# Query low parts in 128-row columns, and linear-attention outputs by pairs of chunks

## The reference, cut to what matters

```python
scores = jnp.einsum('bhtk,bhsk->bhts', q_rel, k_rel)
scores = jnp.where(causal, scores, 0.0)
o = (jnp.einsum('bhts,bhsv->bhtv', scores, vi)
     + jnp.einsum('bhtk,bhkv->bhtv', qi * jnp.exp(b), state))
new_state = (jnp.exp(b_end[..., 0, :])[..., None] * state
             + jnp.einsum('bhsk,bhsv->bhkv', k_end, vi))
```

```python
s = jnp.einsum('bqhd,bshd->bhqs', qb, kk).astype(jnp.float32) * scale
...
a = probs(qb1, k1) - lam * probs(qb2, k2)
return jnp.einsum('bhqs,bshv->bqhv', a.astype(v.dtype), v)
```

## Time and profile before

| | us |
|---|---|
| median of 3 runs | 3016.75 |
| lowest, highest | 3014.66, 3020.86 |
| the profiled execution | 3015.33 |
| its span, first to last instruction | 3013.4 |
| TensorE busy | 2768.4 (92%) |
| VectorE busy | 1497.1 (50%) |
| ScalarE busy | 1224.0 (41%) |
| GpSimd busy | 580.2 (19%) |

### The profile page before, as it was taken

The page is one execution under the profiler, slowest core; times in us unless marked ns, Lnnn a source line. Parts: engine busy times, 40 slices in busy tenths (PEclk is TensorE's granted clock), DMA queues, the critical chain, the costliest instruction groups (busy, mean ns, idle before and its releaser), DMA issues. The chain is left out here.

```text
span 3013.4 us, 36775 instructions
## 1 busy us (share of the span) xinstructions
PE 2768.4 (92%) x13602; PEld 2274.7 (75%) x13602; DVE 1497.1 (50%) x2280; ACT 1224.0 (41%) x1954; POOL 580.2 (19%) x479
## 2 busy tenths in 40 slices
PE   7999999988988599999996699689998999999999
PEld 6887766766767588888885688578876888888887
DVE  4670363456422588888885768456624211221121
ACT  4111243555522278777774411466523312222130
POOL 3222111100221012222221322000022322222221
PEclk9999999999999599999998899799999999999999
DMA  4133124210532299999995511000031211111112
GB/s 149 49 99 114 46 69 130 85 32 24 160 121 97 110 359 376 392 380 372 375 367 207 176 50 32 15 1 1 1 112 56 61 52 49 49 42 56 49 49 77
DMA packets 139399, 380.18 MB, mean 126 GB/s; under 512 B 25984, under 2 KB 49280, under 8 KB 114688
## 3 DMA queue, kind: packets, MB, share of 16 engines
q1 hardware_dynamic: 122032, 344.76, 32.8%
q0 software_dynamic: 10656, 20.99, 2.0%
q10 hardware_dynamic: 6576, 12.58, 1.2%
HBM read 346.81 MB, written 49.28 MB: 131 GB/s over the span
## 5 line engine op out<-in xcount | busy, mean ns | idle before, releaser
L412 POOL TENSOR_TENSOR w_lo<-w_raw,w_hi 128x512 fp32r<-128x512 f32 (+2 forms) x312 | 390.1, 1255 | 1576.4 <-ACT w_hi L387 1575.5
L387 ACT ACTIVATE w_hi<-w_raw 128x512 fp32r<-128x512 f32 (+2 forms) x312 | 184.3, 601 | 975.0 <-PE banks L461 947.4
L2142 DVE TENSOR_TENSOR w_lo<-w_raw,w_hi 128x2048 fp32r<-128x2048 f32 x192 | 436.5, 2290 | 65.8 <-ACT w_hi L2078 60.4
L2078 ACT ACTIVATE w_hi<-w_raw 128x2048 fp32r<-128x2048 f32 x187 | 355.9, 1926 | 39.3 <-PE banks L2199 39.3
L461 PE MATMUL banks<-w_hi,act_hi 128*128 128x512 f32 (+1 forms) x768 | 295.6, 385 | 22.9 <-POOL w_lo L412 10.6
L461 PE MATMUL banks<-act_hi,w_hi 128*128 128x512 f32 x768 | 300.8, 392 | 8.6 <-DVE act_lo L266 3.7
L461 PE MATMUL banks<-act_lo,w_hi 128*128 128x512 f32 x768 | 299.6, 390 | 0.0
L461 PE MATMUL banks<-act_hi,w_lo 128*128 128x512 f32 x768 | 299.5, 390 | 0.0
L461 PE MATMUL banks<-w_hi,act_lo 128*128 128x512 f32 (+1 forms) x768 | 294.4, 383 | 0.0
L461 PE MATMUL banks<-w_lo,act_hi 128*128 128x512 f32 (+1 forms) x768 | 294.4, 383 | 0.0
L2197 PE MATMUL banks<-w_hi,xT 128*128 128x512 f32 x512 | 205.9, 402 | 1.4 <-DVE xT L2147 1.4
(11 more groups left out here) (462 smaller groups left out, 5214.7 us busy)
## 6 DMA issues: line engine op xcount, KB each, us to landing
w_raw<-in_w SPq DMA_DIRECT2D x192, 1024.0 KB, 7.6
w_raw<-in_w_in SPq DMA_DIRECT2D x96, 256.0 KB, 2.7
w_raw<-in_w_up SPq DMA_DIRECT2D x72, 256.0 KB, 2.8
w_raw<-in_w_down SPq DMA_DIRECT2D x64, 256.0 KB, 2.8
scratch_gateT<-gate_staged SPq DMA_DIRECT2D x32, 256.0 KB, 2.2
gate<-scratch_gateT SPq DMA_DIRECT2D x32, 256.0 KB, 3.4
w_raw<-in_w_out SPq DMA_DIRECT2D x32, 256.0 KB, 3.3
y_rows<-scratch_y SPq DMA_DIRECT2D x8, 1024.0 KB, 8.9
```

The lines of the kernel that those rows point to most:

```text
L387: act.activation(v.w_hi[:, i % RING, :cols], v.w_raw[:, i % RING, :cols], ACT.Copy).then_inc(hi_done, 1)
L412: pool.tensor_tensor(v.w_lo[:, i % RING, :cols], v.w_raw[:, i % RING, :cols], v.w_hi[:, i % RING, :cols].bitcast(F32), ALU.subtract).then_ ...
L2078: act.activation(hi[c % SLOTS][:, :], raw[c % TILES][:, :], ACT.Copy).then_inc(hi_done, 1)
L2142: dve.tensor_tensor(lo[c % SLOTS][:, :], raw[c % TILES][:, :], hi[c % SLOTS][:, :].bitcast(F32), ALU.subtract).then_inc(lo_done, 1)
```

## The change

In the differential attention `q_lo` gets the layout of `q_dup`: for each side a full 128-row column in which the other side's 64 rows are zero. The second matmul of `split_scores` then takes 128 rows of `q_lo` and of `k_both`; the rows that would meet the keys' low part are multiplied by zero. POOL writes the zeros in four memsets (64 partitions x 512 elements each, one waiting for the other) at the start of the stage, before its gate subtractions, and the first scores of blocks 0 and 1 wait for them. The larger `q_lo` takes room from the row buffers: one slot instead of two, so only block 0's rows are loaded in the stage before, block 1's at the stage's start after block 0 is turned, and block i + 2's after block i + 1 is turned.

In the linear attention the outputs go by pairs of chunks: both score matmuls, then both state matmuls, where it was score, state, score, state.

```diff
-    v.dq_rows = at("dq_rows", FREE + 103, [P, 2, DA_W])
-    v.dk_rows = at("dk_rows", FREE + 107, [P, 2, DA_W])
+    v.dq_rows = at("dq_rows", FREE + 107, [P, DA_W])
+    v.dk_rows = at("dk_rows", FREE + 109, [P, DA_W])
...
-                    for c in range(8 * half, 8 * half + 8):
-                        r, tt = chunk_rows(c), c // 2
-                        out = v.bank[6 + half][r, (tt % 4) * P:(tt % 4 + 1) * P]
-                        mm = pe.matmul(out, scT[r, h % 2, tt, :], v.hv[r, tt, hc], start=True, stop=(c == 0))
-                        if c:
-                            pe.wait_ge(state_done, NCH * h + c)
-                            mm = pe.matmul(out, q_dec[h % 2][:, c * CHUNK:(c + 1) * CHUNK], st[:, c - 1, :], start=False, stop=True)
+                    mine = range(8 * half, 8 * half + 8)
+                    for tt in range(4 * half, 4 * half + 4):
+                        pair = (2 * tt, 2 * tt + 1)
+                        for c in pair:
+                            r = chunk_rows(c)
+                            pe.matmul(out_of(c), scT[r, h % 2, tt, :], v.hv[r, tt, hc], start=True, stop=(c == 0))
+                        for c in pair:
+                            if c:
+                                pe.wait_ge(state_done, NCH * h + c)
+                                mm = pe.matmul(out_of(c), q_dec[h % 2][:, c * CHUNK:(c + 1) * CHUNK], st[:, c - 1, :], start=False, stop=True)
...
-    q_lo = [at(f"q_lo{i}", q_at[i] + 4, [P, DA_H, P], F32R) for i in range(2)]
+    q_lo = [at(f"q_lo{i}", q_at[i] + 4, [P, 2, DA_H, P], F32R) for i in range(2)]
...
-                if h == 2 and i + 2 < NT:
-                    t = i + 2
-                    sp.wait_ge(tr_ready, 2 * i + 2)
-                    sp.dma_start(v.dq_rows[:, t % 2, :], d["dq"][t * P:(t + 1) * P, :]).then_inc(v.rows_in[t % 2], 16)
-                    sp.dma_start(v.dk_rows[:, t % 2, :], d["dk"][t * P:(t + 1) * P, :]).then_inc(v.rows_in[t % 2], 16)
+                t = i + 2 if h == 2 else 1
+                if p == 0 or h == 2 and t < NT:
+                    sp.wait_ge(tr_ready, 2 * t)
+                    sp.dma_start(v.dq_rows[:, :], d["dq"][t * P:(t + 1) * P, :]).then_inc(v.rows_in, 16)
+                    sp.dma_start(v.dk_rows[:, :], d["dk"][t * P:(t + 1) * P, :]).then_inc(v.rows_in, 16)
...
         def _(pool):
+            for i in range(2):
+                for a in range(2):
+                    pool.memset(q_lo[i][half_rows(1 - a), a, :, :].bitcast(F32), 0.0).then_inc(q_zero, 1)
+                    pool.wait_ge(q_zero, 2 * i + a + 1)
             for b in range(HG_BLOCKS, GATE_BLOCKS):
                 gates.low(pool, b)
...
-                    dve.tensor_tensor(q_lo[t % 2][r, :, :], heads(LOW, r), q_dup[t % 2][r, a, :, :].bitcast(F32), ALU.subtract).then_inc(q_low, 1)
+                    dve.tensor_tensor(q_lo[t % 2][r, a, :, :], heads(LOW, r), q_dup[t % 2][r, a, :, :].bitcast(F32), ALU.subtract).then_inc(q_low, 1)
...
+                if h == 0 and i < 2:
+                    pe.wait_ge(q_zero, 2 * i + 2)
...
-                    r = half_rows(a)
-                    split_scores(pe, v, v.pair[a], q_dup[i % 2][:, a, h, :], k_both[:, a, h, :], q_lo[i % 2][r, h, :], k_both[r, a, h, :],
+                    split_scores(pe, v, v.pair[a], q_dup[i % 2][:, a, h, :], k_both[:, a, h, :], q_lo[i % 2][:, a, h, :], k_both[:, a, h, :],
                                  (i + 1) * P).then_inc(scored, 1)
```

More of the change, by code:

```diff
@@ L800, in hgrn_stage @@
     hog_in = [sem(f"hog_in{i}") for i in range(HG_H)]
-    v.hg_kept, v.rows_in = sem("hg_kept"), [sem(f"qk_rows_in{i}") for i in range(2)]
+    v.hg_kept, v.rows_in = sem("hg_kept"), sem("qk_rows_in")
     FILL = [(84, 10, 16, 10, 12)] + 3 * [(20, 10, 16, 10, 12)]
@@ L827, in _ @@
                 if b == HG_BLOCKS - 2:
-                    for t in range(2):
-                        sp.dma_start(v.dq_rows[:, t, :], d["dq"][t * P:(t + 1) * P, :]).then_inc(v.rows_in[t], 16)
-                        sp.dma_start(v.dk_rows[:, t, :], d["dk"][t * P:(t + 1) * P, :]).then_inc(v.rows_in[t], 16)
+                    sp.dma_start(v.dq_rows[:, :], d["dq"][0:P, :]).then_inc(v.rows_in, 16)
+                    sp.dma_start(v.dk_rows[:, :], d["dk"][0:P, :]).then_inc(v.rows_in, 16)
                 for n in (2 * b, 2 * b + 1):
@@ L1070, in chunk_rows, with out_of @@
                 return slice(c % 2 * CHUNK, c % 2 * CHUNK + CHUNK)
+            def out_of(c):
+                return v.bank[6 + c // 8][chunk_rows(c), c // 2 % 4 * P:(c // 2 % 4 + 1) * P]
             for h in range(HG_H):
@@ L1148, in diff_attention_stage @@
     probs = at("probs", FREE + 80, [P, 2, 2, S])
-    small = FREE + 30
+    small = FREE + 104
     lam = at("lam", small, [P, 4])
@@ L1155, in diff_attention_stage @@
     v.out_gains = at("out_gains", CONST + 6.125, [P, 2])
-    lam_in = at("lam_in", FREE + 102, [P, 4, DA_D])
+    lam_in = at("lam_in", FREE + 106, [P, 4, DA_D])
     lam_pr = at("lam_pr", CONST + 6.25, [P, 2, DA_D])
     link, lam_loaded, lam_dot, lam_exp = sem("dve_link"), sem("lam_loaded"), sem("lam_dot"), sem("lam_exp")
+    q_zero = sem("q_lo_zero")
     tr_ready, q_split, k_high, q_low, k_low = sem("tr_ready"), sem("q_hi"), sem("k_hi"), sem("q_lo"), sem("k_lo")
@@ L1363, in prepare @@
             def prepare(t):
-                pe.wait_ge(v.rows_in[t % 2], 32 * (t // 2 + 1))
+                pe.wait_ge(v.rows_in, 32 * (t + 1))
                 for bank, src in ((LOW, v.dq_rows), (HIGH, v.dk_rows)):
                     for h in range(DA_H):
-                        mm = pe.transpose(bank[:, h * P:(h + 1) * P], src[:, t % 2, h * P:(h + 1) * P], v.ident[:, :])
+                        mm = pe.transpose(bank[:, h * P:(h + 1) * P], src[:, h * P:(h + 1) * P], v.ident[:, :])
                     mm.then_inc(tr_ready, 1)
```

## The result

The changed kernel takes 2973.92 us in the median of 4 runs (2969.98 to 2977.6), the kernel before 3017.39 us (3014.66 to 3020.86). The ratio is 0.985, 95% interval 0.9835 to 0.9865: 43.5 us less, where 40.7 us less and a time of 2976 us were forecast. The profiled execution took 2977.6 us with a span of 2975.7 us.

The account below looks back on a forecast made before the run. TensorE was taken to bound both stages. Outputs 18.2 plus scores 27, less 1 and 0.5 for chains, 1 for start and 2 for clock, gave 40.7 us less: 2976 us, range 2967 to 2984, eight in ten 2966 to 2990.

Parts of the forecast that it names:

- What bounds the kernel: Linear and differential attention both go at TensorE's pace, which pays wherever 64-row and 128-row stationary tiles follow each other.
- Outputs by pairs: Linear attention: 28 pairs of chunks each save 0.65 us, so the stage ends 18.2 us sooner (16 to 19.6).
- the two answers for the state pair: Linear attention's two state matmuls: 0.37 us if like the score pair, 0.50 us if not overlapping; 0.42 us taken.
- Scores in 128 rows: Differential attention: 0.27 us saved per one-bank side, 0.65 us per two-bank side; 27 us taken (0 to 30).
- Chains: Differential attention: waits on other engines' work take back 1 us in blocks 4 to 6 and 0.5 us in block 7.
- Start: Start of the differential attention: memsets ahead of POOL's subtractions may delay the first scores; 1 us lost (0 to 3.7).
- Clock: Differential attention, less dense: one or two more stretches of lowered granted clock, 2 us lost (gain 2 to lose 6).
- Sum: Whole kernel: all gains less losses give 40.7 us, so a time of 2976 us (2967 to 2984).
- B: Differential attention scores: full-height tiles load no sooner than half-height ones, scores gain nothing; gain 17 us, time 3000; chance 0.04.
- C: Linear attention outputs: pairs don't run together, every step costs 0.36 us a matmul; gain 22.5 us, time 2994; chance 0.06.
- D: Differential attention, blocks 0 to 7: more gaps keep the clock at half over much of it, slower than before; chance 0.03.
- A: Differential attention, blocks 4 to 7: chains set the pace once scores are short; gain 31 us, time 2986; chance 0.18.

Follow-up runs that it names:

- e6: Changed kernel with each output step's two matmuls in the same rows and columns (chunks 0 and 2, then 1 and 3); 2988.27 us.
- e5: Changed kernel without the second matmul of the differential attention's scores (low query part times keys left out); 2962.56 us.

## Why the prediction was right, step by step

- **What bounds the kernel**: right. TensorE sets the pace in both stages. The linear attention shrank by 18.8 to 19.4 of 19.9 us, the scores by 27.6 of 29.9 us at like clock.
- **Outputs by pairs**, 18.2 us: measured 28 x 0.71 = 19.9 us on TensorE, 18.8 to 19.4 in the stage. Of the two answers for the state pair the cheap one was true, 0.37 and not 0.42 us. The dear one was mis-sized: e6 has 0.58 us for a pair that cannot overlap, and I had 0.50, since I took a pass of 128 columns at twice the 0.036 us spacing of the head's scores. Those were themselves two column tiles side by side. That ACT's gate copy comes 0.68 us late in head 0 was not seen.
- **Scores in 128 rows**, 27 us: the two rows gave 29.4 us, which I lowered for the sides of 128 keys. The sides, start to mask, measured 29.9 us (0.24, 0.29, 0.29, 0.28, 0.62, 0.68, 0.67, 0.67 us a side from block 0 to 7, times 8). The rows of the other attention had carried the price to 0.02 us, and the cut was unfounded.
- **Chains**, 1.5 us: right place, too small. TensorE's idle time in blocks 4 to 7 is 9.2 us in all three profiles of the old scores and 11.3 to 12.2 us in the new ones, 2 to 3 us more. The stall ahead of the row turn stayed as long as it was, as argued (1.82, 1.65 and 1.97 us in blocks 4 to 6). The unit after it kept only 0.54, 0.30 and 0.27 us of some 1.3 us, where 1 us of loss was put on all three; in block 6 part of that is clock, since in all old profiles a stretch of half clock stands in the unit ahead. The prediction saw DVE's maximum late there; what TensorE waits for is the same split one step earlier, since the bank that it turns into is read by it. TensorE's and DVE's rows of unit (6, 2) in the changed kernel:

```profile
660.74 1.41 DVE L1318 TENSOR_TENSOR k_both<-banks,k_both 64x512 fp32r<-64x512 f32 x2
...
662.25 0.96 PE L1409 MATMUL banks<-ident,probs 128*128 128x128 f32 x7 [0.87 <-issue]
```

  In block 7 the units lost their 1.35 us each in full.
- **Start**, 1 us: 2.0 to 2.5 us in the changed kernel, and for another reason. The memsets took 2.25 us, as estimated. DVE's product was held, as the prediction feared, but only by the first subtraction, which the memsets had moved beside it; it ended 4.78 us after the first turn where it was 4.83 us before. What was added is the clock, which turned eleven filler matmuls of 0.23 us into 0.43 us.
- **Clock**, 2 us lost: wrong in sign for the scores. The kernel before had 0.98 and 0.97 there, the changed one 1.00, 189.2 and 189.1 us. The prediction saw one stretch of half clock, at 649; there were three. Without any, the old scores would have some 216 us by an estimate from 1.6 us for each. That the new ones have fewer is what 13 profiles show; no run shows why.
- **Sum.** By the stages the change gives 19.1 us (mean of two profiles each) and 28.2 us, 47 us together; by the medians 43.5 and 44.1. With the scores at like clock it is 19.1 + 27.6 and some 2.2 us less for the start, 44.5 us, so most of the gap is the clock of the profiled executions. The forecast of 40.7 came out near because its misses offset each other, which is partly luck: the gains of outputs and scores were put 4 us too low, the losses to chains and start some 2 us too low, and the scores lost nothing to the clock where 2 us stood. The lower end of the eight in ten, 2966 us, does not follow from its words: no clock loss and full pairs give 2976 - 2 - 1.4 = 2972.6.
- **Rivals.** B fell with the load at 658.87, C with the four steps of 0.37 us, D with the clock. B's rule, from "TensorE: Matmul & The Clock Gate", Part 3, of the Trainium skill, that a load overlaps a running matmul only in other row groups, does not hold in this kernel: q_lo's 128 rows load under a matmul of 128 rows. The same part of the Trainium skill also lets a load run ahead into a background weight buffer, which the prediction left out and which this load would fit. A did not set in, and even e5, with 11.5 us less work in blocks 4 to 7, loses only about 2.3 us of it to other engines.

## What to carry to other kernels

Look at the distance of starts and at when weights are loaded, not at busy time: where stationary tiles of 64 rows and tiles of 128 rows alternate, each change costs time that no row names, only an idle weight loader held by "issue". Filling half-height tiles with zeros cost TensorE nothing here: a side of 512 and 384 keys took 0.90 us with 128 rows where it took 1.57 us with 64. Where small tiles are wanted, do many of one size in a row, and put neighbours into different rows and columns, or different columns where they use all rows. And before a difference of two profiles is put down to a change, compare the granted clock of the two stretches.

## What the runs showed of the hardware

- A float32 matmul of 128 columns in two passes costs 0.22 us in the same tile and 0.01 us more in another tile of the same size; the tiles 64x64 at opposite corners and 128x64 side by side behave alike.
- A change between these sizes costs 0.14 us beside that.
- A 96-row tile behaves as a full one (0.55 and 0.91 us a bank and a side).
- DVE's product of two SBUF operands ended 0.15 us after the POOL subtraction that ran when it began, in all 13 profiles, whether it had waited 0.6 or 2.1 us for it. DVE's subtractions from PSUM were not held (1.40 us for two in all kernels), and POOL's memsets held nothing up that could be seen.
- A stretch of half clock of 3.4 us cost the stage 1.6 us in the old scores and 0.6 us in the new ones: with the memsets last, unit (6, 1) took 9.45 us instead of the changed kernel's 7.83, and the unit behind it, which has a wait to give up, 4.91 instead of 5.97.
